# A triangular inverse in a decoder step: two of four matrices moved to the off-diagonal 64x64 tiles

## What is computed

```
a_mat = jnp.where(strict, jnp.einsum('bhnid,bhnjd->bhnij', kb, k) * decay, 0.0)
t_mat = lax.linalg.triangular_solve(a_mat + eye, eye, left_side=True, lower=True)
u = t_mat @ (v * beta[..., None])
w = t_mat @ (kb * jnp.exp(gc)[..., None])
```

## Time and profile before

| | us |
|---|---|
| Three runs, median (lowest to highest) | 2949.26 (2948.16 to 2951.23) |
| The profiled execution, first to last instruction | 2949.0 |
| TensorE busy in it | 2917.4 (99%) |
| VectorE, ScalarE, GpSimd busy | 1780.6, 1410.9, 172.0 |

### The profile page before, as it was taken

The page is one execution under the profiler, slowest core; times in us unless marked ns, Lnnn a source line. Parts: engine busy times, 40 slices in busy tenths (PEclk is TensorE's granted clock), DMA queues, the critical chain, the costliest instruction groups (busy, mean ns, idle before and its releaser), DMA issues.

```text
span 2949.0 us, 68978 instructions
## 1 busy us (share of the span) xinstructions
PE 2917.4 (99%) x25560; PEld 2839.8 (96%) x25560; DVE 1780.6 (60%) x2823; ACT 1410.9 (48%) x2104; POOL 172.0 (6%) x268
## 2 busy tenths in 40 slices
PE   7999999999999999999999999999999999999999
PEld 7999999999999999999999999999999999999999
DVE  6778778778776555555555444577555555554444
ACT  6556556556554444444444333555444444444433
POOL 0212112112120000000000000000000000000000
PEclk9999999999999999999999999999999999999999
DMA  7565656555656665555555656743555555555655
GB/s 213 172 183 164 186 172 177 176 160 174 179 158 183 195 188 175 180 181 180 178 179 181 181 168 180 215 153 120 155 174 181 180 178 179 182 180 178 180 173 150
DMA packets 520520, 518.92 MB, mean 176 GB/s; under 512 B 31808, under 2 KB 443625, under 8 KB 520089
## 3 DMA queue, kind: packets, MB, share of 16 engines
q1 hardware_dynamic: 518574, 510.21, 57.5%
q0 software_dynamic: 1152, 5.58, 0.6%
q10 hardware_dynamic: 594, 0.25, 0.0%
HBM read 491.99 MB, written 32.82 MB: 178 GB/s over the span
## 4 chain that ended last, share of the span: by engine, by line
PE 68%; DVE 0%; issue 0%; ACT 0%; DVEq 0%; ACTq 0%
PE bank L480 22%; PE bank L482 22%; PE bank L481 22%; PE bank L1035 0%; PE bank L1011 0%; PE bank L1047 0%; PE bank L1023 0%; PE bank L1037 0%; PE bank L588 0%; PE bank L1148 0%; PE bank L1070 0%; PE bank L1012 0%; PE bank L1025 0%; DVE w_lo L468 0%; DVE x_res L2457 0%
## 5 line engine op out<-in xcount | busy, mean ns | idle before, releaser
L468 DVE TENSOR_TENSOR w_lo<-w_raw,w_hi 128x1024 fp32r<-128x1024 f32 x858 | 1049.0, 1223 | 950.5 <-ACT w_hi L461 947.8
L461 ACT ACTIVATE w_hi<-w_raw 128x1024 fp32r<-128x1024 f32 x858 | 908.6, 1059 | 1318.4 <-PE bank L482 1317.0
L480 PE MATMUL bank<-h_hi,w_hi 128*128 128x264 f32 x4624 | 1353.1, 293 | 8.9 <-DVE w_lo L468 7.0
L482 PE MATMUL bank<-h_hi,w_lo 128*128 128x264 f32 x4624 | 1314.6, 284 | 0.0
L481 PE MATMUL bank<-h_lo,w_hi 128*128 128x264 f32 x4624 | 1314.6, 284 | 0.0
L480 PEld LDWEIGHTS bank<-h_hi,w_hi 128*128 128x128 f32 x4624 | 872.4, 189 | 31.4 <-issue 11.6
L481 PEld LDWEIGHTS bank<-h_lo,w_hi 128*128 128x128 f32 x4624 | 874.3, 189 | 1.3
L482 PEld LDWEIGHTS bank<-h_hi,w_lo 128*128 128x128 f32 x4624 | 872.5, 189 | 0.0
L480 PE MATMUL bank<-a_hi,w_hi 128*128 128x264 f32 x1408 | 401.3, 285 | 4.8 <-DVE w_lo L468 2.6
L481 PE MATMUL bank<-a_lo,w_hi 128*128 128x264 f32 x1408 | 402.1, 286 | 0.0
L482 PE MATMUL bank<-a_hi,w_lo 128*128 128x264 f32 x1408 | 401.4, 285 | 0.0
(11 more groups left out here) (382 smaller groups left out, 2645.5 us busy)
## 6 DMA issues: line engine op xcount, KB each, us to landing
w_raw<-in_w_gate_up_dram SPq DMA_DIRECT2D x704, 256.0 KB, 2.9
w_raw<-in_w_in_a_dram SPq DMA_DIRECT2D x388, 256.0 KB, 3.2
w_raw<-in_w_down_dram SPq DMA_DIRECT2D x352, 256.0 KB, 3.2
w_raw<-in_w_out_a_dram SPq DMA_DIRECT2D x128, 256.0 KB, 3.3
s_dec<-in_state_delta_dram SPq DMA_DIRECT2D x32, 512.0 KB, 5.4
out_dram<-s_dec SPq DMA_DIRECT2D x32, 512.0 KB, 5.1
w_raw<-in_w_q_b_dram SPq DMA_DIRECT2D x64, 256.0 KB, 3.0
w_raw<-in_w_o_b_dram SPq DMA_DIRECT2D x64, 256.0 KB, 3.1
```

Source lines behind the costliest of these rows:

```text
L461: nc.scalar.activation(w_hi[:, s % SPL, :], w_raw[:, s, :], ACT.Copy).then_inc(hi_ready, 1)
L468: ops.tensor_tensor(w_lo[:, s % SPL, :], w_raw[:, s, :], w_hi[:, s % SPL, :].bitcast(F32), ALU.subtract).then_inc(lo_ready, 1)
L480: nc.tensor.matmul(bank[bk][:, 0:T], wh, xh, start=first, stop=False)
L482: m = nc.tensor.matmul(bank[bk][:, 0:T], wl, xh, start=False, stop=last)
```

## The change

PSUM banks 4 to 7 become one tensor `upper`, of which `pair01` and `pair23` are the first 128 columns of two neighbouring banks each. A product now puts matrices 0 and 1 in the first bank of a pair and matrices 2 and 3 in the second. For matrices 2 and 3 the result of block b goes to the partitions of the other block, so that a product uses four pairs of input rows and output rows: 0 to 0, 0 to 1, 1 to 1, 1 to 0, in this order, twice over. With each product the two blocks of matrices 2 and 3 change places, and the first U of GpSimd is made in three instructions so that they start in the right one.

In place of U + P^2 U the kernel computes (I + P^2) U in one product. VectorE makes I + P^2 and I + P^4 (`Fm`, the buffer of `Xm`) with `plus`, and I + P^8 straight from PSUM. ScalarE now copies U out of PSUM three times. The count of products and of matmuls stays.

```diff
-        bank = [ctx.enter_context(nc.psum_tensor(f"bank{i}", [P, 512], F32)) for i in range(8)]
+        lower = [ctx.enter_context(nc.psum_tensor(f"bank{i}", [P, 512], F32)) for i in range(4)]
+        upper = ctx.enter_context(nc.psum_tensor("upper", [P, 4, 512], F32))
+        bank = lower + [upper[:, i, :] for i in range(4)]
         B = bank[4:]
+        pair01, pair23 = upper[:, 0:2, 0:P], upper[:, 2:4, 0:P]
+
+        def twos(t):
+
+            return t[:, :, :].rearrange("p (a m) n -> p a (m n)", a=2)
...
-                sqn, oT, rhs, UF = norm_sq, norm_h, vn, NT
+                sqn, oT, rhs, UF, Fm = norm_sq, norm_h, vn, NT, Xm
...
 
                 pool.wait_ge(inv_dve, 15 * G + 1)
-                pool.tensor_tensor(Um[:, :, :], bc(ident_h, 1, 4), PaT[:, :, :], ALU.subtract).then_inc(um_ready, 1)
+                pool.tensor_tensor(Um[:, 0:2, :], bc(ident_h, 1, 2), PaT[:, 0:2, :], ALU.subtract).then_inc(um_ready, 1)
+                for b in range(2):
+                    at, to = slice(HP * b, HP * (b + 1)), slice(HP * (1 - b), HP * (2 - b))
+                    pool.wait_ge(um_ready, 3 * G + (1 + b))
+                    pool.tensor_tensor(Um[to, 2:4, :], bc(ident_h[at, :], 1, 2), PaT[at, 2:4, :], ALU.subtract
+                                       ).then_inc(um_ready, 1)
+                pool.wait_ge(um_ready, 3 * G + 3)
...
-                elif n in (4, 5, 6):
-                    dst, bk, k = {4: (Pb, 0, 1), 5: (Pa, 2, 2), 6: (Pb, 1, 4)}[n]
-                    act.wait_ge(inv_pe, 13 * G + k)
-                    nc.scalar.activation(dst[:, :, :], B[bk][:, 0:2 * P], ACT.Copy).then_inc(inv_act, 1)
+                elif n == 4:
+                    act.wait_ge(inv_pe, 13 * G + 1)
+                    nc.scalar.activation(twos(Pb), pair01, ACT.Copy).then_inc(inv_act, 1)
+                elif n == 5:
+                    act.wait_ge(inv_pe, 13 * G + 2)
+                    nc.scalar.activation(twos(Pa), pair23, ACT.Copy).then_inc(inv_act, 1)
+                    act.wait_ge(inv_pe, 13 * G + 3)
+                    nc.scalar.activation(twos(Um), pair01, ACT.Copy).then_inc(inv_act, 1)
+                elif n == 6:
+                    act.wait_ge(inv_pe, 13 * G + 5)
+                    nc.scalar.activation(twos(Um), pair01, ACT.Copy).then_inc(inv_act, 1)
                 elif n == 7:
+                    act.wait_ge(inv_pe, 13 * G + 6)
+                    nc.scalar.activation(twos(Um), pair23, ACT.Copy).then_inc(inv_act, 1)
...
             def each4(out, lhsT, rhs_):
 
-                for m_ in range(4):
+                for i in range(2):
                     for b in range(2):
-                        mm = nc.tensor.matmul(out[block(b), m_ * HP:(m_ + 1) * HP], lhsT(m_, b), rhs_(m_, b),
-                                              start=True, stop=True)
+                        for m_ in (i, i + 2):
+                            to = block(b if m_ < 2 else 1 - b)
+                            mm = nc.tensor.matmul(out[to, m_ // 2, i * HP:(i + 1) * HP], lhsT(m_, b), rhs_(m_, b),
+                                                  start=True, stop=True)
...
-                inv = lambda s, k: pe.wait_ge(s, (7 if s is inv_act else 15) * G + k)
+                inv = lambda s, k: pe.wait_ge(s, (9 if s is inv_act else 15) * G + k)
...
                     inv(inv_dve, 2)
                     pe.wait_ge(st_copied, G + 1)
-                    each4(B[0], half(PaT), half(Pa)).then_inc(inv_pe, 1)
+                    pe.wait_ge(k_copied, G + 1)
+                    each4(pair01, half(PaT), half(Pa)).then_inc(inv_pe, 1)
                 elif n == 5:
                     inv(inv_act, 1)
-                    inv(inv_dve, 3)
+                    inv(inv_dve, 4)
+                    pe.wait_ge(v_copied, G + 1)
                     pe.wait_ge(intra_ready, G + 1)
-                    pe.wait_ge(um_ready, G + 1)
-                    each4(B[2], half(PbT), half(Pb)).then_inc(inv_pe, 1)
-                    each4(B[0], half(Pb), half(Um)).then_inc(inv_pe, 1)
+                    pe.wait_ge(um_ready, 3 * G + 3)
+                    each4(pair23, half(PbT), half(Pb)).then_inc(inv_pe, 1)
+                    each4(pair01, half(Fm), half(Um)).then_inc(inv_pe, 1)
                 elif n == 6:
                     inv(inv_act, 2)
-                    inv(inv_dve, 4)
-                    pe.wait_ge(k_copied, G + 1)
-                    each4(B[1], half(PaT), half(Pa)).then_inc(inv_pe, 1)
                     inv(inv_dve, 5)
-                    each4(B[2], half(Pa), half(Um)).then_inc(inv_pe, 1)
-                elif n == 7:
+                    each4(pair23, half(PaT), half(Pa)).then_inc(inv_pe, 1)
                     inv(inv_act, 3)
                     inv(inv_dve, 6)
-                    pe.wait_ge(v_copied, G + 1)
-                    each4(B[3], half(Pb), half(Um)).then_inc(inv_pe, 1)
+                    each4(pair01, half(Fm), half(Um)).then_inc(inv_pe, 1)
+                elif n == 7:
+                    inv(inv_act, 4)
+                    inv(inv_dve, 7)
+                    each4(pair23, half(Pb), half(Um)).then_inc(inv_pe, 1)
                     for m_ in range(4):
                         m = nc.tensor.transpose(B[0][:, m_ * P:(m_ + 1) * P], NT[:, m_, :], ident)
                     m.then_inc(inv_pe, 1)
                 elif n == 8:
 
-                    inv(inv_act, 4)
-                    inv(inv_dve, 7)
-                    each4(B[1], full(Nm), half(Um)).then_inc(inv_pe, 1)
+                    inv(inv_act, 6)
+                    each4(pair23, full(Nm), half(Um)).then_inc(inv_pe, 1)
                 elif n == 10:
                     inv(inv_dve, 9)
-                    each4(B[2], half(Tm), half(Xm)).then_inc(inv_pe, 1)
+                    each4(pair01, half(Tm), half(Xm)).then_inc(inv_pe, 1)
                 elif n == 11:
...
                     turned = lambda dst, src: nc.vector.transpose(dst[:, :, :], src[:, :, :]).then_inc(inv_dve, 1)
-                    add = lambda dst, bk, op: tt(dst[:, :, :], dst[:, :, :], m4(B[bk][:, 0:2 * P]), op).then_inc(inv_dve, 1)
-                    msk = lambda bk, lv: tt(Xm[:, :, :], m4(B[bk][:, 0:2 * P]), bc(lv, 1, 4), ALU.mult).then_inc(inv_dve, 1)
+                    plus = lambda dst, src: tt(dst[:, :, :], src[:, :, :], bc(ident_h, 1, 4), ALU.add).then_inc(inv_dve, 1)
+                    a2 = lambda ap: ap.rearrange("p (a m) n -> p a m n", a=2)
+                    b2 = lambda ap: ap.rearrange("p a (m n) -> p a m n", m=2)
+                    m22 = lambda ap: bc(bc(ap, 1, 2), 1, 2)
                     if n == 4:
-                        dve.wait_ge(inv_act, 7 * G + 1)
+                        dve.wait_ge(inv_act, 9 * G + 1)
                         turned(PbT, Pb)
+                        plus(Fm, Pb)
                     elif n == 5:
-                        dve.wait_ge(inv_act, 7 * G + 2)
+                        dve.wait_ge(inv_act, 9 * G + 2)
                         turned(PaT, Pa)
                         got(3)
-                        add(Um, 0, ALU.add)
+                        plus(Fm, Pa)
                     elif n == 6:
-                        got(5)
-                        own(5)
-                        add(Um, 2, ALU.add)
+                        got(4)
+                        tt(a2(Pb[:, :, :]), b2(pair23), m22(ident_h), ALU.add).then_inc(inv_dve, 1)
                     elif n == 7:
-                        got(6)
-                        own(6)
-                        add(Um, 3, ALU.add)
-                        own(7)
-                        turned(Tm, Um)
+                        dve.wait_ge(inv_act, 9 * G + 5)
+                        nc.vector.transpose(Tm[:, 0:2, :], Um[:, 0:2, :])
+                        for b in range(2):
+                            at, to = slice(HP * b, HP * (b + 1)), slice(HP * (1 - b), HP * (2 - b))
+                            m = nc.vector.transpose(Tm[to, 2:4, :], Um[at, 2:4, :])
+                        m.then_inc(inv_dve, 1)
                     elif n == 8:
                         got(8)
-                        msk(1, lvl16_h)
+                        tt(a2(Xm[:, :, :]), b2(pair23), m22(lvl16_h), ALU.mult).then_inc(inv_dve, 1)
                     elif n == 10:
                         got(9)
-                        own(7)
-                        add(Um, 2, ALU.subtract)
+                        tt(twos(Um), twos(Um), pair01, ALU.subtract).then_inc(inv_dve, 1)
                         own(10)
                         turned(Tm, Um)
                     elif n == 11:
```

More of the change, by code:

```diff
@@ L1968, in step @@
                 elif n == 13:
-                    inv(inv_act, 5)
+                    inv(inv_act, 7)
                     inv(inv_dve, 13)
@@ L1978, in step @@
                 elif n == 14:
-                    inv(inv_act, 6)
+                    inv(inv_act, 8)
                     inv(inv_dve, 15)
@@ L1986, in step @@
                 elif n == 15:
-                    inv(inv_act, 7)
```

(5 more changed lines are left out.)

## The result

| | before | after |
|---|---|---|
| Median (lowest to highest), four runs each | 2949.52 (2948.16 to 2951.23) | 2927.67 (2927.00 to 2929.88) |
| The profiled execution, first to last instruction | 2949.0 | 2925.2 |

The account below looks back on a forecast made before the run. TensorE, busy 2917.4 of 2949.0 us, was taken as the bound. Shorter products at steps 5 and 6 (0.45 us each) and 7, 8, 10 (0.22 each), step 4 at 0, save 1.56 us x 16 turns = 25.0: 2924 us, range 2919 to 2929.

## What to carry to other kernels

When work is added to an engine off the critical path, look at what runs on its neighbour at that moment, not only at when the result is needed: three GpSimd instructions in place of one, with microseconds to spare, took a sixth of the gain by running into a VectorE instruction that TensorE waited for. A saving ahead of a stall that another engine sets is worth nothing until the stall is moved, and the move is often only an order: here two swaps of neighbouring instructions gave 10 us on top, and the second was found only because the first had been made and a new wait of 0.3 us stood in its place. Where products are smaller than the array, put them on all its tiles in turn: here this took a product from 0.68 to 0.46 us, and the same tile twice running cost 0.05 us.

## What the runs showed of the hardware

- Four fp32 matmuls of 64x64 on the four pairs of input and output sides, into two banks, run side by side: a product of eight takes 0.46 us, against 0.68 on the two diagonal tiles in turn and 0.73 on these two when each is used twice running.
- GpSimd and VectorE held each other up where VectorE's instruction had two inputs in SBUF (the split, `qdec`) and GpSimd's read SBUF too. With GpSimd's 64x128 instruction begun first, VectorE's split went from 1.22 to 1.48 us; with the split begun first it kept 1.22, and GpSimd's pair went from 1.07 to 1.85 us; in the changed kernel `kq_diag`, begun inside the split, went from 0.21 to 1.07 us. An overlap of 0.14 us at the split's start left it at 1.22, one of 0.39 made it 1.48, and one of 0.42 made it 1.50. The Trainium skill, SBUF — State Buffer, section "SBUF: two separate sides", describes this as a lock on a shared pair of ports that whoever starts first holds for the whole instruction, also for a VectorE instruction with two inputs in SBUF against a GpSimd one that reads SBUF. The trace agrees: `kq_diag` ended 0.07 us behind the split, and the split's extra 0.26 us lie within the 0.39 us in which the two overlapped. In all three cases the split's delay is 0.13 to 0.14 us short of the overlap; why is not shown.
